# A hybrid mixer written as one order of steps: a projection group inside each of the first nine head turns, and a six-slot weight ring

## What is computed

```python
for l in range(2):
    mod = silu(c) @ ada_w[l] + ada_b[l]              # 12 pieces of 512 columns: shifts, scales, gates
    h = rmsnorm(x) * (1 + sc1) + sh1
    m_qk, m_v, m_o, m_if, f_q, f_k, f_v, f_f, s_q, s_k, s_v, n_q, n_kv, n_g = split(h @ w_in[l])
    y_a = mlstm(...)      # gated linear memory, with a causal convolution on q and k
    y_b = fox(...)        # softmax attention with a forget bias
    y_c = stick(...)      # stick-breaking attention: softplus, suffix sums, exp
    y_d = nsa(...)        # compressed blocks + "sel" + "win" softmax attention
    x = x + g1 * (concat(y_a, y_b, y_c, y_d) @ w_out[l])
    h = rmsnorm(x) * (1 + sc2) + sh2
    x = x + g2 * (swiglu(h) if l == 0 else top2_of_8_experts(h))
```

## Time and profile before

| | |
|---|---|
| median of 3 runs | 1823.13 us (1821.71 to 1824.36) |
| profiled execution, its own time | 1818.27 us |
| span in the trace | 1816.4 us |
| mixer of layer 0, from the end of the gates' product to the end of `wout` | 49.7 to 284.9 us |
| head turns of layer 0 and of layer 1 | 150.0 to 249.6 us, 650.6 to 754.4 us |
| FFN of layer 0 | 294.0 to 545.2 us |
| mixer of layer 1, the same way | 558.2 to 789.8 us |
| norm, router and experts of layer 1 | 789.8 to 1816.4 us |

### The profile page before, as it was taken

How to read it: one execution, slowest core, us unless ns; L and a number is a source line. 1 busy time by engine, 2 the same in 40 slices (tenths; PEclk the granted TensorE clock), 3 DMA queues, 4 the chain that set the end, 5 groups by cost and what they waited for, 6 DMA issues and landing times.

```text
span 1816.4 us, 17209 instructions
## 1 busy us (share of the span) xinstructions
PE 1703.1 (94%) x6820; PEld 941.6 (52%) x6820; DVE 499.2 (27%) x1011; ACT 209.7 (12%) x467; POOL 1.1 (0%) x8
## 2 busy tenths in 40 slices
PE   2999888999998998979999999999899999999997
PEld 2567654545545676654445444454344454444543
DVE  6585552434413145442111011110001110111102
ACT  1101321000012113211001000010000010000100
POOL 0000000000000000000000000000000000000000
PEclk8996579999999975679999999999999999999999
DMA  9996002686883000009998999989978989999893
GB/s 350 335 343 221 1 2 102 231 249 242 300 291 111 30 1 1 1 33 394 391 365 330 390 387 362 371 320 392 389 270 327 381 329 390 386 364 370 321 391 146
DMA packets 221795, 481.65 MB, mean 265 GB/s; under 512 B 15592, under 2 KB 33384, under 8 KB 221712
## 3 DMA queue, kind: packets, MB, share of 16 engines
q1 hardware_dynamic: 220264, 478.64, 71.8%
q10 hardware_dynamic: 1448, 1.84, 0.3%
HBM read 479.41 MB, written 1.06 MB: 265 GB/s over the span
## 4 chain that ended last, share of the span: by engine, by line
PE 85%; DVE 3%; issue 3%; DMA 3%; PEld 2%; SPq 2%; ACT 1%; DVEq 0%; ACTq 0%
PE bank L1021 26%; PE bank L1050 14%; PE bank L1016 11%; PE bank L797 6%; PE bank L1042 6%; PE bank L788 3%; PE bank L997 3%; PE bank L1095 2%; PE bank L1028 1%; DMA ring<-in_moe_wu 1%; DMA ring<-in_ada_w 1%; PEld bank L1021 1%; PE bank L1111 1%; PE bank L857 1%; PE bank L871 1%
## 5 line engine op out<-in xcount | busy, mean ns | idle before, releaser
L1021 PE MATMUL bank<-ring,h_T 128*128 128x512 f32 (+1 forms) x896 | 362.1, 558 | 15.5 <-issue 8.9
L1050 PE MATMUL bank<-ring,m_qk_T 128*128 128x512 f32 x624 | 277.7, 597 | 0.7 <-ACT m_qk_T L668 0.7
L1021 PEld LDWEIGHTS bank<-ring,h_T 128*128 128x128 f32 x896 | 170.3, 194 | 181.9 <-issue 130.2
L1021 PE MATMUL bank<-ring,cmp_region 128*128 128x512 f32 x448 | 197.1, 593 | 0.0
L1050 PEld LDWEIGHTS bank<-ring,m_qk_T 128*128 128x128 f32 x624 | 116.2, 190 | 144.8 <-issue 140.9
L1551 DVE SCALAR_TENSOR_TENSOR m_s_region<-s_v,bank 128x512 f32<-128x512 f32 (+1 forms) x70 | 39.1, 559 | 464.4 <-ACT s_v L661 464.4
L661 ACT ACTIVATE s_v<-bank 128x512 f32<-128x512 f32 (+1 forms) x70 | 34.6, 494 | 986.6 <-PE bank L1021 654.4
L1021 PEld LDWEIGHTS bank<-ring,cmp_region 128*128 128x128 f32 x448 | 83.6, 190 | 99.1 <-issue 99.1
L1228 DVE SCALAR_TENSOR_TENSOR ada_acc<-ring,cond,ada_acc 128x512 f32<-128x512 f32 x168 | 126.3, 752 | 6.0
L1555 DVE SCALAR_TENSOR_TENSOR m_s_region<-m_s_region,bank 128x512 f32<-128x512 f32 (+1 forms) x70 | 39.1, 558 | 320.3 <-PE bank L1021 225.0
L797 PE MATMUL bank<-ring,h_T 128*128 128x512 f32 (+1 forms) x320 | 113.2, 509 | 0.9 <-PE bank L797 0.3
(11 more groups left out here) (373 smaller groups left out, 1194.5 us busy)
## 6 DMA issues: line engine op xcount, KB each, us to landing
ring<-in_moe_wg SPq DMA_DIRECT2D x56, 2048.0 KB, 9.5
ring<-in_moe_wu SPq DMA_DIRECT2D x56, 2048.0 KB, 14.3
ring<-in_moe_wd SPq DMA_DIRECT2D x56, 2048.0 KB, 18.7
ring<-in_ada_w SPq DMA_DIRECT2D x24, 2048.0 KB, 14.6
ring<-in_w_in SPq DMA_DIRECT2D x10, 2048.0 KB, 15.3
ring<-in_ffn_wg SPq DMA_DIRECT2D x6, 1536.0 KB, 12.1
ring<-in_ffn_wu SPq DMA_DIRECT2D x6, 1536.0 KB, 14.0
ring<-in_ffn_wd SPq DMA_DIRECT2D x6, 1536.0 KB, 14.7
```

What stands on the lines that cost most here:

```text
L1021: last = mm(ps[4 + part][:, 0:w], xT[st.into][:, k, 128 * st.tile:128 * st.tile + 128], slot_view(n, w)[:, k, :], start=k == 0, stop=k == ...
L1050: last = mm(ps[st.y + half][:, :], hbT[:, j % 2, 128 * q:128 * q + 128], slot_down(st.loads[2], st.w)[:, q, 512 * half:512 * half + 512], ...
```

## The change

One function, `mixer_order`, writes the mixer of a layer as a single sequence, from which PE, ACT and DVE each take their own steps. The head kinds come in the order sel, win, mLSTM, fox, stick; the groups in the order gates, 5, 6, 0, 1, 2, 3, 4. Gates, pieces 5 and 6 and half of a group of piece 0 come ahead of the turns, around `compress`. In turn s PE does `second(s-1)`, `first(s)`, `third(s-2)` and, in turns 0 to 8, one whole projection group; the other eleven turns have none. Probabilities and scores have two buffers instead of four. `wout` is cut into pieces by pairs of k, which run in turns 17 to 21 and after. `compress` alternates its two products. Before the experts the ring has six slots; the seventh holds the normalised q and k and other mixer tensors, since `h_T` now stays in use. `ada` pieces 10 and 11 of layer 0 move into the FFN, which now has 14 pieces in its seven units. ACT instead of PE frees a `win` slot.

```diff
-GROUPS = [(None, 0)] + [(c, g) for c in range(6) for g in range(2)] + [(6, g) for g in range(3)]
+GROUPS = [(None, 0)] + [(5, g) for g in range(2)] + [(6, g) for g in range(3)] + [(c, g) for c in range(5) for g in range(2)]
...
-HEADS = [(k, h) for k in ("mlstm", "fox", "stick", "sel", "win") for h in range(H)]
+HEADS = [(k, h) for k in ("sel", "win", "mlstm", "fox", "stick") for h in range(H)]
...
+    proj(0)
+    dve("gates")
+    act("gate_ln")
+    proj(1, 0, 1)
+    dve("gate_rows")
+    modulation(4)
+    pe("gate_T")
+    dve("gate_cols")
+    act("gates_exp")
+    proj(2, 0, 1)
+    if l == 0:
+        pe("bias_T")
+        dve("bias")
+    modulated(*((4,) if l == 0 else (10, 11)))
+    proj(3)
+    modulation(5)
+    proj(4)
+    dve("cmpx")
+    proj(5)
+    dve("nsa_ss")
+    act("rstd", "nsa")
+    dve("nsa_norm")
+    pe("proj", 6, 0)
+    modulated(*((5,) if l == 0 else ()))
+    pe("compress")
+    dve("nsa_gates")
+    modulation(6)
+    pe("nsa_T")
+    pe("proj", 6, 1)
+    act("evac", 6)
...
+    fill = [(7, 0, 1), (8,), (9,), (10,), (11,), (12,), (13,), (14, 0, 1), (15, 0, 1)]
+    for s in range(NH + 2):
+        if 1 <= s <= NH:
+            pe("second", s - 1)
+            dve("part2", s - 1)
+            if HEADS[s - 1][0] == "stick":
+                act("stick_exp", s - 1)
+        if s < NH:
+            pe("first", s)
+            if HEADS[s][0] == "stick":
+                act("softplus", s)
+            dve("part1", s)
+            if HEADS[s][0] != "stick":
+                act("exp", s)
+        if s >= 2:
+            pe("third", s - 2)
+        if s < len(fill):
+            proj(fill[s][0], *fill[s][1:])
...
+        elif s == 1:
+            dve("kv_cols")
+            pe("cmp_scores")
+            dve("cmp_shift")
+            act("cmp_exp")
+            modulation(7)
+        elif s == 2:
+            dve("cmp_probs")
+            pe("cmp_turn")
...
+        elif s == 6:
+            act("tanh")
+            dve("mqk")
+            modulation(9)
...
+        elif s == 9:
+            dve("finish", 1)
+        elif s == 10:
+            dve("fox_ss")
+            act("rstd", "fox")
+            dve("fox_norm")
+        elif s == 11:
+            for a in range(2):
+                pe("fox_T", a)
+                dve("fox_cols", a)
+        elif s == 13:
+            dve("finish", 2)
+            act("rstd", "mlstm")
+            dve("mlstm_end")
+        elif s == 16:
+            pe("mix_T", 0)
+            act("mix_cols", 0)
+            pe("mix_T", 1)
+            dve("mix_cols", 1)
+        elif s == 17:
+            dve("finish", 3)
+            pe("wout", 0, 0, (0, 1))
+        elif s == 18:
+            pe("mix_T", 2)
+            act("mix_cols", 2)
+            pe("wout", 1, 0, (0, 1))
+        elif s == 19:
+            pe("wout", 0, 1, (0, 1, 2))
+        elif s == 20:
+            pe("wout", 1, 1, (0, 1))
+        elif s == 21:
+            pe("wout", 0, 0, (2,))
+            dve("finish", 4)
+            pe("wout", 1, 0, (2,))
+            pe("mix_T", 3)
+            dve("mix_cols", 3)
+            pe("wout", 1, 1, (2,))
+    for half, tt in ((0, 0), (1, 0), (0, 1), (1, 1)):
+        pe("wout", half, tt, (3,))
...
+SEQ = [(0,) + k for k in ADA[:4] + WINS[:2] + ADA[4:5] + WINS[2:3] + ADA[5:6] + WINS[3:4] + ADA[6:7] + WINS[4:5] + ADA[7:8]
+       + WINS[5:6] + ADA[8:9] + WINS[6:] + ADA[9:10] + WOUT]
+
+ADA_FFN = [(0, 10), (0, 11)] + [(1, c) for c in range(12)]
...
+PRE = RING - 1
...
-            return i % RING
+            return i % PRE
...
-                    for j in range(32):
-                        mm(ps[6][0:NCMP, 0:DH], cmpx[0:DH, j, :], cmpw[0:DH, j, :], start=j == 0, stop=j == 31)
-                    for j in range(32):
-                        last = mm(ps[7][0:DH, 0:NCMP], cmpw[DH:128, j, :], cmpx[DH:128, j, :], start=j == 0, stop=j == 31)
...
+                    for j in range(32):
+                        mm(ps[1][0:DH, 0:NCMP], cmpw[DH:128, j, :], cmpx[DH:128, j, :], start=j == 0, stop=j == 31)
+                        last = mm(ps[2][0:NCMP, 0:DH], cmpx[0:DH, j, :], cmpw[0:DH, j, :], start=j == 0, stop=j == 31)
```

More of the change, by code:

```diff
@@ L79 @@
 N_B, N_P, N_STICK = count(BKINDS, NH), count(PKINDS, NH), H
[L80 to L117, removed]
@@ L134 @@
+FREED = FILLED[:PRE] + [1]
+assert LOADS % RING == 0
 class Step:
@@ L650, in swiglu @@
+                for engine, (step, *at) in ORDER[l]:
+                    if engine == "act":
+                        does[step](*at)
             def swiglu(f, steps, base, do, after=lambda j: None):
@@ new lines, in mixer @@
+                does = {"proj": proj, "gate_T": gate_transposes, "bias_T": bias_turn, "ada": lambda c: ada_reduce(l, c), "compress": compress,
+                        "nsa_T": nsa_transposes, "kv_T": kv_transposes, "cmp_scores": compressed_scores, "cmp_turn": cmp_turn,
+                        "cmp_out": cmp_product, "fox_T": fox_transposes, "first": first, "second": second, "third": third,
+                        "mix_T": mix_transposes, "wout": wout}
+                for engine, (step, *at) in ORDER[l]:
+                    if engine == "pe":
+                        does[step](*at)
@@ L1527, in cmp_take @@
+                def cmp_take():
                     dve.wait_ge(cmp_out, l + 1)
[L1528 to L1531 removed]
@@ new lines, in mixer @@
+                does = {"gates": gates, "gate_rows": gate_running, "gate_cols": gate_columns, "bias": bias_tiles, "conv": convolve, "mqk": silu_qk,
+                        "ada_sum": lambda c, k: ada_sum(0, c, k), "ada_take": modulation_taken, "fox_ss": fox_squares, "fox_norm": fox_scale,
+                        "fox_cols": fox_columns, "cmpx": compress_inputs, "nsa_ss": nsa_squares, "nsa_norm": nsa_scale, "k_cmp": k_compressed,
+                        "kcn": k_scaled, "nsa_cols": nsa_columns, "kv_cols": kv_columns, "nsa_gates": nsa_gates, "cmp_shift": cmp_exponents,
+                        "cmp_probs": cmp_weights, "cmp_turned": cmp_turned, "cmp_take": cmp_take, "part1": part1, "part2": part2,
+                        "finish": finish, "mlstm_end": finish_mlstm, "mix_cols": mix_columns}
@@ new lines, in mixer @@
+                for engine, (step, *at) in ORDER[l]:
+                    if engine == "dve":
+                        does[step](*at)
+                for n, (half, tt) in enumerate(((0, 0), (1, 0), (0, 1), (1, 1))):
+                    dve.wait_ge(wout_done, 4 * l + n + 1)
+                    if tt:
+                        dve.sem_inc(ring_free[slot_of(AT[(l, "wout", half)])], 1)
+                    xs = x[:, tt, 512 * half:512 * half + 512]
+                    do(TTop(wide[:, 0:512], ps[((3, 6), (7, 4))[half][tt]][:, :], gate[:, 0, 512 * half:512 * half + 512], ALU.mult))
+                    do(TTop(xs, xs, wide[:, 0:512], ALU.add), x_mixed if half == 1 else None)
```

762 lines of the change are left out of this document (412 added, 350 removed).

## The result

The changed kernel took 1835.22 us (median of 4 runs, 1833.58 to 1837.07), the kernel before on the same chip 1823.54 us (1821.71 to 1824.36). The ratio is 1.0066, with a 95% interval of 1.0048 to 1.0083: slower by 12 us. The forecast was 1814.7 us, with 1804 to 1826 as its own range. The changed kernel's profiled execution took 1833.89 us (span 1832.1), 15.6 more than the profiled 1818.27 of before.

A forecast was written before the change was run, and what follows sets the result against it. It took the head turns to be bound by TensorE at half speed. Layer 0 -5.0, layer 1 -13.2 and FFN +9.8 on 1818.27 gave 1809.9 us (1814.7 against the median); own range 1804 to 1826, with rivals 1797 to 1838.

The forecast's parts named there:

- three terms: Changes against the kernel before: layer 0's mixer -5.0 us, layer 1's mixer -13.2, the FFN +9.8.
- The step that failed first: compress: Ahead of the first turn: alternated products partly overlap, 8.6 us plus 1.4 for the clock, 10.0; bounds 7.0 and 14.0.
- It ends as group 2 ends, so I count no wait.: Ahead of layer 0's first turn: VectorE's 6 us `ada` piece 4, before the gate columns, makes TensorE wait 0.
- the wait of turn 8: Layer 0: `second` waits for an exponential behind mqk and piece 9 on VectorE, 4.2 us late.
- the wait of turn 2: Layer 0: cmp_turn waits behind cmp_shift, piece 7, part2, part1 and cmp_probs on VectorE, 1.9 us late.
- hand-overs: Between projection groups in turns 0 to 8: nine times 0.3 us added in each layer.
- Turns 16 to 21 and wout: Stick turns with the wout pieces: 48.2 us in each layer, turn 17 taking 9.6 with 2.0 for the rising clock.
- The FFN's mechanism: Loads need the earlier `wd` slot: 2.5 us over five units, 5.4 more at the fourth, reductions 1.9; +9.8.
- The clock stayed low in the fox turns: Answers a rival, chance 0.12: clock stays at 2.4 GHz in turns 12 to 17, 10.3 us less per layer, 1794.
- the six-slot ring's waits: Rival, chance 0.13: `wd` slot frees only after the next `up`, each FFN unit 5.5 us late, +25 more, 1840.
- the clock was up in wout: Answers a rival, chance 0.07: clock stays low through the wout pieces, 18 us more in each layer, 1851.
- the turns kept to their chain: Answers a rival, chance 0.18: the eleven turns without groups cost 1 us more for each of eight, 16 more, 1831.

The follow-up runs named there:

- x1: The changed kernel with its two compress products in two runs, one after the other, instead of alternating: 1819.1 us, 0.9984 of the kernel before.
- x5: The kernel before with its two compress products alternated instead of one after the other: 1838.4 us, 1.0085 of the kernel before.
- x12: The changed kernel with its two compress products alternated in runs of eight: 1822.2 us, 1.0 of the kernel before.
- x2: The changed kernel with the gate columns ahead of the sums of `ada` slice 4, whose reduction goes behind group 3: 1829.6 us.
- x3: The changed kernel with seven ring slots for slices, the seventh's tensors moved to `x_norm` and `ada_acc`: 1819.9 us, 1.0001 of the kernel before.
- x8: The changed kernel with compress products one after the other, gate columns first and a seven-slot ring: 1801.9 us, 0.9887 of the kernel before.
- x9: The changed kernel with groups 7 and 8 whole in turns 0 and 1, groups 9 to 15 in halves over turns 2 to 15: 1805.2 us.

## Why the prediction was wrong

It put three terms against 1818.27: -5.0, -13.2 and +9.8. They came out as +8.6, -11.5 and +14.5, with 3.3 more in the experts and 0.7 between the stages. The change was forecast to be faster and was slower.

**The step that failed first: compress.** "When they alternate, a record with the long stream can lie over the other's long load", 10.0 us, with bounds of 7.0 and 14.0. It took 18.2, above both. Both bounds came from the 7.00 us runs of the earlier trace rows, which ran at 1.2 GHz, for a stretch that was otherwise counted at 2.4; there the two products, apart, take 7.5 us (x1). So the price of the order that the kernel already had was nearly twice too high, and left as it was it would have been cheaper than the 10.0 forecast for alternating. The upper bound, "no overlap", also left out that a change from one product to the other could itself cost something; x5 and x12 show that it does. Of layer 0's 18.2 us 7.5 are the products at 2.4 GHz, 6.1 the changes (64 x 0.096, the difference of 0.213 and 0.117 us a product), and 4.6 the clock, which fell to 1.2 GHz after 4.5 us. The Trainium skill's rule (page "TensorE: Matmul & The Clock Gate", Part 3) that such products in different row groups run concurrently would have made it 7.0 by the forecast's rows and some 3.9 by those of x1; these runs disagree, with 18.2 us alternated and 7.5 apart.

**"It ends as group 2 ends, so I count no wait."** The work of VectorE was right (5.47 us for the seven), its start was not: the slice landed at 63.8, 7.15 us after VectorE was ready for it, because of the very ring that the FFN part had priced. It cost 6.0 us of waiting and 2.4 of slow product. x2 and x3 took it away, each in its way. The forecast looked at what the change does to the ring in the FFN only.

**The head turns held, in part by luck.** Turns 0 to 8 of layer 0 took 89.1 us (forecast 88.8), with the wait of turn 8 at 4.63 (4.2). But the wait of turn 2, put at 1.9, was 0.17, and the 2.7 of hand-overs don't show; in their place some 5 us went to records at a lower clock than forecast (0.94 for 1.0), in turn 2 (a group of 8.78 us for 7.13) and behind the wait of turn 8. Turns 9 to 11 took 15.4 (15.0; the terms written there add up to 15.4); the fox turns 29.8 (29.9), at 1.2 GHz as taken. Turns 16 to 21 and wout took 44.0 for 48.2: turn 17, put at 9.6, took 6.0, since the clock was up before its wout piece. In layer 1 turns 0 to 8 took 75.2 for 78.9: the nine hand-overs of 0.3 don't show. With compress apart and the wait gone, x8 has 46.7 and 45.0 us ahead of the turns for the 48.3 and 46.4 forecast, with compress at 7.6 for 10.0; so the other terms of that sum were 0.8 and 1.0 us short.

**The FFN's mechanism was right, its size not.** The fourth unit's wait was 9.79 us, 5.25 more than before (forecast 5.4). The other four waits were 3.9 in all (2.5). The rest of the 14.5 us, 5.3, is PE's own: 1.7 in reductions (1.9), and 3.6 in the gate and up products. Of these 2.7 lie behind the two longest waits, where the clock was 0.63 and 0.80: 8.44 us for 7.58 before, and 8.83 for the 7.03 that a group of 512 columns takes at 2.4 GHz. The price of a wait's clock, counted elsewhere in the prediction, was left out here.

**Of the rivals** none came as written. The clock stayed low in the fox turns, outside the fourth unit the six-slot ring's waits were 0.2 to 2.3 us a unit and not 5.5, the clock was up in wout, and the turns kept to their chain. But the ring was the second cause: with seven slots 15.4 us go (x3), part of them ahead of the turns, where the forecast didn't look for it. The first is compress, 16.1 us by x1, a term for which no rival stood. Neither alone explains the sign: x1 and x3 each end level with the kernel before (0.9984 and 1.0001), and with both mended, and the gate columns, the kernel is clearly faster (x8, 0.9887). That 1835.2 lies inside the wide range of 1797 to 1838 is luck in the main: its upper end stood for a ring that is late at every unit. The books, between the profiled executions: the forecast of 1809.9 was 24.0 us short of 1833.9. Compress is 16.4 of this in the two layers, the late slice 8.4, the FFN 4.7, the experts and the gaps 4.0: 33.5, from which 9.5 come off for turns and wout that took less than forecast, net of small overruns. (Against the medians the miss is 20.5, since the profiled execution of before lay 4.9 us under its median and that of after 1.3.) Why the experts took 3.3 us more stays open.

**What the change got right** is smaller than what it left. As an order of turns it puts nine groups whole into nine turns and none into eleven, and the eleven then ran at 0.50 to 0.63 of the clock where they aren't stick turns. The prediction priced these bare turns well, and didn't ask what they would cost with half a group each: x9 shows 30 us.

## What to carry to other kernels

When two series of small products are to be interleaved, bound the cost above "no overlap": here a change from one to the other cost 0.10 us beside a product of 0.12. Take a row's price only with the clock at which it ran. Spread the long products that need nobody over all the turns that wait for other engines, in halves if need be, rather than giving some turns more than their wait holds and others none; read the clock by stretch to find the bare ones. A ring with one slot less is paid wherever its queue is tight, so follow it from the first load on, and count each wait of TensorE with the slower products behind it.
